# Three feed-forward blocks whose gate and up products are done in 2x2 blocks with seven products instead of eight

## What is computed

```python
def conv_ffn(h, w_up, conv_w, conv_b, w_down):       # layers 0 and 1
    u, g = jnp.split(h @ w_up, 2, axis=-1)
    g = causal_dwconv(g, conv_w, conv_b)
    return (jax.nn.silu(g) * u) @ w_down
# layer 2
h2 = rmsnorm_2(x, norm2_g[l])
g = jnp.einsum('bsd,df->bsf', h2, w_gate[l])
u = jnp.einsum('bsd,df->bsf', h2, w_up[l])
x = x + jnp.einsum('bsf,fd->bsd', jax.nn.silu(g) * u, w_down[l])
```

## Time and profile before

| | us |
|---|---|
| median of 3 runs (lowest, highest) | 1824.26 (1824.08, 1824.57) |
| span of the profiled execution, first to last instruction | 1822.8 |
| PE busy | 1810.1 (99%) |
| DVE busy | 938.6 (51%) |
| ACT busy | 727.8 (40%) |
| POOL busy | 272.3 (15%) |

### The profile page before, as it was taken

One profiled execution on the slowest core, in us unless ns is written; L12 is line 12 of the kernel. 1 busy time (PEld: TensorE's weight loads), 2 busy tenths in 40 slices (PEclk: granted clock), 3 DMA queues, 4 the chain that ended last, 5 costly groups with the idle time before them and its releaser, 6 DMA issues.

```text
span 1822.8 us, 21331 instructions
## 1 busy us (share of the span) xinstructions
PE 1810.1 (99%) x8733; PEld 1472.7 (81%) x8733; DVE 938.6 (51%) x1429; ACT 727.8 (40%) x1155; POOL 272.3 (15%) x241
## 2 busy tenths in 40 slices
PE   9999999999999999999999999999999999999998
PEld 7877788888888887878888888877777888888886
DVE  6878556443453456545653345458667443333324
ACT  5644444331332435654432233332567432212223
POOL 2001222210121200002221022103001222101210
PEclk9999999999999999999999999999999999999999
DMA  6121123222222333212223222232121132222221
GB/s 243 67 88 66 70 95 114 93 93 94 91 95 96 118 128 108 82 47 93 93 95 113 93 93 95 91 110 99 70 103 59 70 109 100 93 92 93 102 89 64
DMA packets 32337, 173.41 MB, mean 95 GB/s; under 512 B 4064, under 2 KB 6240, under 8 KB 14320
## 3 DMA queue, kind: packets, MB, share of 16 engines
q1 hardware_dynamic: 26848, 162.55, 25.0%
q10 hardware_dynamic: 5392, 9.51, 1.6%
HBM read 169.38 MB, written 2.13 MB: 94 GB/s over the span
## 4 chain that ended last, share of the span: by engine, by line
PE 96%; ACT 1%; DVE 1%; DMA 0%; POOL 0%; issue 0%; SPq 0%; ACTq 0%; DVEq 0%; POOLq 0%
PE ps L995 54%; PE ps L1299 20%; PE ps L929 7%; PE ps L1014 5%; PE ps L1141 2%; PE ps L1186 2%; PE ps L1166 2%; PE ps L1034 1%; PE ps L1225 1%; PE ps L1206 1%; DMA raw<-in_wall 0%; ACT PC L1543 0%; DVE WL L1806 0%; ACT WH L1375 0%; POOL sq L2326 0%
## 5 line engine op out<-in xcount | busy, mean ns | idle before, releaser
L995 PE MATMUL ps<-hH,WH 128*128 128x512 f32 x1456 | 570.9, 392 | 0.1
L1806 DVE TENSOR_TENSOR WL<-raw,WH 128x1024 fp32r<-128x1024 f32 (+2 forms) x308 | 377.3, 1264 | 368.1 <-ACT WH L1375 367.9
L995 PE MATMUL ps<-hH,WL 128*128 128x512 f32 x1456 | 566.7, 389 | 0.0
L995 PE MATMUL ps<-hL,WH 128*128 128x512 f32 x1456 | 566.7, 389 | 0.0
L1375 ACT ACTIVATE WH<-raw 128x1024 fp32r<-128x1024 f32 (+2 forms) x308 | 301.4, 1026 | 311.8 <-PE ps L1299 228.6
L995 PEld LDWEIGHTS ps<-hH,WH 128*128 128x128 f32 x1456 | 273.3, 188 | 65.3 <-issue 7.3
L995 PEld LDWEIGHTS ps<-hH,WL 128*128 128x128 f32 x1456 | 273.3, 188 | 57.0
L995 PEld LDWEIGHTS ps<-hL,WH 128*128 128x128 f32 x1456 | 273.3, 188 | 56.9 <-issue 1.0
L1299 PE MATMUL ps<-fL,WH 128*128 128x512 f32 x531 | 205.9, 388 | 0.0
L1299 PE MATMUL ps<-fH,WL 128*128 128x512 f32 x531 | 205.9, 388 | 0.0
L1299 PE MATMUL ps<-fH,WH 128*128 128x512 f32 x531 | 205.9, 388 | 0.0
(11 more groups left out here) (369 smaller groups left out, 2020.7 us busy)
## 6 DMA issues: line engine op xcount, KB each, us to landing
raw<-in_wall SPq DMA_DIRECT2D x140, 1024.0 KB, 4.6
...
```

What stands on the lines that cost most here:

```text
L995: mm = e.matmul(ps[b][:, 0:N], ww[:, k, c:c + 128], x[:, k, 0:N], start=(k == 0 and i == 0), stop=(k == 7 and i == 2))
L1806: e.tensor_tensor(WL[n % NCV][:, c], raw[n % NRAW][:, c], WH[n % NCV][:, c].bitcast(F32), ALU.subtract).then_inc(*mark("wl", n, x))
```

## The change

From the second pair of tiles on (s = 1 to 10; s = 0 stays as it was) the gate and up tiles of an FFN are computed together as a 2x2 block product. The rows of the block are gate and up (256 features each), the inner dimension is split into the even and the odd tiles of k (four each), and the columns are the tokens 0 to 255 and 256 to 511. Seven products of half size (PRODUCTS = 1, 5, 6, 3, 7, 2, 4) take the place of eight. A product is 4 k tiles x 2 output tiles x 3 passes = 24 matmuls of 128 x 256.

- **Sums of weights.** Weights come in chunks of 1024 columns (half a unit). Four of the seven products (5, 6, 3, 7) need sums or differences of chunks: DVE adds them (`wsum`) before ACT and DVE split the sum into H and L (`cconv`). Four chunks fit into WH, WL; a chunk may be split when the one four places before it has been used.
- **Sums of activations.** Once for each FFN DVE makes four combinations of scaled X (`wt`, four times), ACT and DVE split them (TH, TL); the one for product 7 goes into hH, hL after the direct pair (`wt7`).
- **Sums of results.** Products 1, 6, 7 and 4 add up in one bank (wA), 5 and 3 in another (wD), 2 has its own (wB). ACT copies the bank out after 1, 5, 6 and 7 (`wcopy`), and PE waits: 6 for the copy of 1, 7 for that of 6, 4 for that of 7, 3 for that of 5. DVE forms the gate (`wc12`, `wc11`), times Rsb over [128, 2, 512] (`wgate`), ACT and DVE do the taps, ACT silu, POOL times Rsb; DVE forms up and multiplies (`wz1`, `wz0`); ACT and POOL make FH and FL, both over [128, 2, 512].
- **Down** is no longer in two halves: after each s one or two pieces of 24 matmuls of 128 x 512 (`wd`), each followed by DVE's adding to X (`wx`), and a tail of the last four tiles.
- **Memory.** A third raw buffer; stages A and B place some tensors elsewhere so that the new ones find room; the fences ahead of the FFNs go.

The diff, cut to what the rest speaks of:

```diff
+WINO = (0, 1, 2)
+PRODUCTS = (1, 5, 6, 3, 7, 2, 4)
...
+def wino_sequence():
+    out = []
+    for s in range(1, NSU):
+        out += [("q", s, q) for q in PRODUCTS] + [("d",) + x for x in down_pieces(s)]
+    return out
...
     def conv_ahead(end):
...
+        while now["conv"] < len(ITEMS):
+            item = ITEMS[now["conv"]]
+            kind, n = item
+            first = n if kind == "unit" else CHUNKS[n]["from"]
+            if first >= end or any((b if b[0] == "chunk" else b[1]) not in done for b in W_BEFORE[item]):
+                return
...
+                for c in range(now["summed"], min(n + 2, len(CHUNKS))):
+                    if CHUNKS[c]["i"] == CHUNKS[n]["i"]:
+                        if CHUNKS[c]["sum"]:
+                            put("wsum", c)
+                        now["summed"] = c + 1
+                put("cconv", n)
...
+                if nrm in WINO_OF and m in (5, 6):
+                    put("wt", WINO_OF[nrm], m - 5)
...
+    def ffn_wino(i, end):
...
+        for p, _ in enumerate(g_fm(1, FFN_NORMS[i], f"g{i}", "wg0")):
+            put("wt", i, 2 + p)
+        for _ in g_fm(1, FFN_NORMS[i], f"u{i}", "wu0"):
+            conv_ahead(len(UNITS))
+        flush_norms()
+        put("wt7", i)
+        for x in SEQUENCE:
+            conv_ahead(len(UNITS))
+            if x[0] == "d":
+                _, g, c = x
+                put("wd", i, g, c)
+                while late:
+                    put(*late.pop(0))
+                used((i, "d", g, c))
+                put("wx", i, g, c)
+                continue
+            _, s, q = x
+            put("wp", i, s, q)
...
+            if q in (1, 5, 6, 7):
+                put("wcopy", i, s, q)
+            elif q == 3:
+                put("wc12", i, s)
+            elif q == 2:
+                put("wc11", i, s)
+                put("wgate", i, s)
+            else:
+                put("wz1", i, s)
+                late.append(("wz0", i, s))
...
+                elif what == "wp":
...
+                    if not opens:
+                        w.wait_ge(*at("wcopy", i, st, {6: 1, 7: 6, 4: 7, 3: 5}[pn]))
+                    w.wait_ge(*at("wl", "c", c))
+                    W = [x.rearrange("p (k c) -> p k c", k=4) for x in chunk_slot(c)]
+                    for p in range(4):
+                        w.wait_ge(*at(*moving_at(i, pn, p)))
+                        H, L = moving(pn, p)
+                        for u in (0, 1):
+                            for n, (ww, x) in enumerate(((W[0], H), (W[0], L), (W[1], H))):
+                                mm = e.matmul(ps[b][:, 256 * u:256 * u + 256], ww[:, p, 128 * u:128 * u + 128], x,
...
+                elif what == "cconv":
+                    c = a[0]
+                    if CHUNKS[c]["sum"]:
+                        w.wait_ge(*at("wg", "sum", c))
...
+                    e.activation(chunk_slot(c)[0], chunk_src(c), ACT.Copy).then_inc(*mark("wh", "c", c))
...
+                elif what == "wz1":
+                    i, st = a
+                    w.wait_ge(*at("wcopy", i, st, 7))
+                    w.wait_ge(*at("wcopy", i, st, 5))
+                    e.tensor_tensor(held_w[:, :, :], held_w[:, :, :], held_q5[:, :, :], ALU.add).then_inc(
...
+                    w.wait_ge(*at("wpool", "y", i, st))
+                    e.scalar_tensor_tensor(out=yz[:, :, 256:512], in0=held_w[:, :, :], scalar=-1.0,
+                                           in1=yz[:, :, 256:512], op0=ALU.mult, op1=ALU.mult).then_inc(
```

More of the change, by code:

```diff
@@ new lines, with weight_places @@
+CHUNKS, ITEMS = chunk_list()
+CHUNK_AT = {c["key"]: n for n, c in enumerate(CHUNKS)}
+def weight_places():
+    at, before, held, pos = {}, {}, {}, 0
+    for item in ITEMS:
+        wide = 2 if item[0] == "unit" else 1
+        pos += pos % wide
+        at[item] = pos % W_SLOTS
+        before[item] = []
+        for x in range(pos, pos + wide):
+            last = held.get(x % W_SLOTS)
+            if last is not None and last not in before[item]:
+                before[item].append(last)
+            held[x % W_SLOTS] = item
+        pos += wide
+    return at, before
@@ L164, in conv_ahead @@
     def conv_ahead(end):
-        while now["conv"] < min(end, len(UNITS)) and (now["conv"] < NCV or now["conv"] - NCV in done):
-            for x in (0, 1):
-                put("conv", now["conv"], x)
+        while now["conv"] < len(ITEMS):
[4 more added lines that the diff above has]
+                return
+            if kind == "unit":
+                for x in (0, 1):
+                    put("conv", n, x)
+            else:
+                for c in range(now["summed"], min(n + 2, len(CHUNKS))):
[4 more added lines that the diff above has]
+                put("cconv", n)
             now["conv"] += 1
@@ L694, in program @@
             top[0] = base
+            if i in WINO and i != 1:
+                continue
             if i == 1:
@@ L763, in col @@
             return cols[p, a:a + n]
-        s_raw = [sem(f"raw{i}") for i in range(NRAW)]
+        s_raw = [sem(f"raw{i}") for i in range(NRAW + 1)]
         s_mem = [sem(f"mem{i}") for i in range(4)]
```

558 lines of the change are left out of this document (518 added, 40 removed).

## The result

The changed kernel takes 1898.89 us at the median of four runs (1896.98 to 1900.32) against 1824.41 (1824.08 to 1824.66): ratio 1.0406, 95% interval 1.0394 to 1.0419. It is slower, as forecast, but by 74.5 us where 47 were put, and outside the range, which ended at 1895. The profiled execution has a span of 1897.1 us.

The account below looks back on a forecast made before the run. PE was taken to bound the kernel. Gains of 48.3 us against waits gave +23.4 in each of FFNs 0 and 1 and -5.0 in FFN 2, together +41.8; with 5 for the clock, 1871 us, range 1812 to 1895.

Parts of the forecast that it names:

- wt among w_out's tiles: Just ahead of an FFN: combinations wt made among w_out's last tiles, put at 0.3 us lost.
- start, products 5 and 6: s = 0 to 1 in FFNs 0 and 1: 6.1 us lost ahead of product 5, 5.7 ahead of product 6.
- s = 1 to 2, 2 to 3: Steps with one down piece in FFNs 0 and 1: 5.7 us lost in each of the two.
- seven passages s >= 3: Steady steps of FFNs 0 and 1: 33.4 us instead of 31.0, about 2.3 lost each, DVE held by POOL.
- Load waits in s = 2 and 3: DVE's sum for the next product 5 waits for its raw unit to land: some 1.5 us late.
- The clock: PE's clock may fall in six start stalls of some 6 us: 0 to 15.4 us, 5 taken.
- FFN 2: The FFN without taps: 11.1 us lost at start and s = 1, 2, 16.1 gained, together -5.0.
- Costed at nothing: Put at 0 us: the tail, covered by 12 + 12 matmuls, the layout of stages A and B, loads and banks.
- B: Rival: POOL's holds fall beside DVE's train of operations; 1817 us, range 1805 to 1830, chance 0.17.
- C: Rival: splitting chunks three or four ahead covers every DVE train; 1776 us, chance 0.08.
- D: Rival: small waits add up without slack, or the clock falls at every stall; 1895 to 1920 us, chance 0.10.
- A: The forecast itself: DVE's train, held by POOL, makes PE wait; 1852 to 1884 us with its bounds, chance 0.60.

Follow-up runs that it names:

- e5: Changed kernel with weight combinations wt 0 and 1 moved behind the FFN's first gate tile, 2 and 3 behind the second: 1896.19 us, ratio 1.0391.
- e8: Changed kernel with 14 extra matmuls of 256 columns ahead of product 5's wait at s = 1: 1900.65 us, ratio 1.0416.
- e6: Changed kernel with only the third FFN in 2x2 blocks, new layout and three raw buffers kept: 1828.17 us, ratio 1.0019.
- e1: Changed kernel with POOL's y (s = 1 to 10) and FL (from s = 4) computed for 16 of 512 tokens, work left out: 1858.1 us.
- e10: Changed kernel with POOL's FL of a step made in the next step, after DVE's split of the down chunk: 1867.6 us, ratio 1.0235.
- e4: Changed kernel with ACT's copies of products 1 and 5 ahead of the weight copies due there: 1889.91 us, ratio 1.0358.
- e9: Changed kernel with POOL's FL as two instructions of 512 instead of one of 1024: 1882.25 us, ratio 1.0316.

## Why the prediction was wrong in size

The direction and the mechanism of the steady step were right, the sum was 27 us short, and the largest term that failed stood at the heads of the FFNs. For FFN 0, beyond PE's own work:

| step of the forecast | forecast | trace |
|---|---|---|
| wt among w_out's tiles | 0.3 | 7.3 (5.0 of pause, the rest clock) |
| start, products 5 and 6 | 11.8 | 9.2 |
| s = 1 to 2, 2 to 3 | 11.4 | 14.7 |
| seven passages s >= 3 | 16.1 | 16.4 |
| together | 39.6 | 47.6 |

- **The step that failed** is "With 0.3 for wt among w_out's tiles". I costed the two combinations by their DVE time and did not walk the queue ahead of the last X and hL: the weight-split pair that stands there too, and the round trips to ACT within a combination (0.9 for TH, with DVE idle). It cost 5.0 us of pause, three times, with the clock behind it 7.3, 7.0 and 8.3 in the first tiles, and 1.4 more ahead of FFNs 1 and 2: 25 us where 0.9 was put. And everything after it (the reciprocal came at 284.6 instead of 277.6) started later. e5 showed that the place alone was not it: put elsewhere, the same work stopped PE there, and only 2.7 us came back. What counts is the amount that stands in one chain ahead of products 1 to 6.
- **Products 5 and 6**: the 6.1 ahead of product 5 was seen as 6.5. The 5.7 ahead of product 6 did not come (PE idle for 0.1, 0.4 and 0.8): the splits for 6 and 3 stand ahead of wt7 and of its L7, which I had put in front. The split for 6 ended at 309.35, 2.3 after product 5's end at full pace, and the half pace of product 5 covered that; e8, with product 5 at full pace, shows the 2.25.
- **Load waits in s = 2 and 3**: 1.5 each was put for them, 3.2 and 2.2 came, so in FFN 0 2.4 of the 3.3 between 11.4 and 14.7 can be theirs; no run separates them.
- **The clock**: 5 us from bounds of 0 to 15.4, with the reason that the one drop seen needed a longer pause. That was misread: in the kernel before PE's last matmul ended at 1815.19, and from 1816.60 on the clock was at 0.50. It fell after every start pause and in s = 2 and 3. Bodies of 5.04, 5.07 and 4.35 us instead of 2.76 make 6.2 in FFN 0, and 2 more in the first tiles. Some 8 in each of FFNs 0 and 1 and 4 in FFN 2 are 20, above my upper bound, since I had counted one product for each of six start pauses, and PE slowed at four places in an FFN. e8 says that not all of it is additional, and no run says how much is.
- **FFN 2**: -5.0 forecast, +2.6 seen. Of the 7.6 between them, 8.3 are the first tiles, where nothing was put; products 5 and 6 cost 5.0, not 7.7, and s = 2 and 3 together 5.2, not 3.4.
- **Costed at nothing**: the tail. My cover argument counted FL for the tail's matmuls and not the chain behind it, X to hH to hL at 2.15 a tile, which the next stage waits for: 6.0 of the 8.7 in stages B and C (the other 2.7 are wt's). e6 rules out the layout, the other thing costed at nothing.
- **The steady step**: 33.4, at a margin of 0.03 in the race between DVE's sum and POOL's FL. DVE came first, and the loss was still 2.3, the upper end of the 1.3 to 2.5 put for that case. So it is in part luck that 33.4 was met to 0.02: 1.7 and 0.6 at ACT's copies were walked; 1.3 for product 6's own held split and 0.9 for the copy of 5 came. e1 and e10 show the cause, e4 the 0.4 of ACT's copy, e9 the size. The gain of PE is as read from the earlier trace rows: 120 ns a matmul, steps of 31.06 in FFN 2.
- **The rivals**: B and C fell with e1 and e10 (the holds were real, 31 us). D, small waits adding up in a chain without slack, with the clock falling at every stall, 1895 to 1920 at 0.10, is what the starts and s = 2 and 3 did, on top of A.

Open: what the clock and the load waits cost by themselves, and whether the chain cut in three in all FFNs, with s = 1 to 3 given more time (a second direct pair), would beat the kernel before there; it wasn't tried. As far as tried, the 2x2 form pays only in the FFN without taps, 4 us of 1825 (0.2%), where its matmuls alone save 16.
